# Second block's norms scaled inside their PSUM banks, next weight slabs split elsewhere, large SBUF buffers at multiples of 512 bytes

## The reference

```python
def layer_norm_2(x, g, b):
    xf = x.astype(jnp.float32)
    mu = jnp.mean(xf, axis=-1, keepdims=True)
    var = jnp.mean(jnp.square(xf - mu), axis=-1, keepdims=True)
    y = (xf - mu) * lax.rsqrt(var + LN_EPS)
    return (y * g.astype(jnp.float32) + b.astype(jnp.float32)).astype(x.dtype)

for l in range(DEPTH_2):
    mix = hybrid_mixer(h, w_in[l], ..., w_out[l], cos, sin)
    h = layer_norm_2(DEEPNORM_ALPHA * h + mix, ln1_g[l], ln1_b[l])
    h = layer_norm_2(DEEPNORM_ALPHA * h + cross_attention(h, mem, cq_w[l], ckv_w[l], co_w[l]),
                   ln2_g[l], ln2_b[l])
    h = layer_norm_2(DEEPNORM_ALPHA * h + swiglu(h, ffn_wi[l], ffn_wo[l]), ln3_g[l], ln3_b[l])
```

## Time and profile before

| | before |
|---|---|
| median of 3 runs | 2712.55 us |
| profiled execution | 2717.11 us |
| its span, first to last instruction | 2715.3 us |
| granted TensorE clock, mean | 0.978 of full speed |
| PE busy | 2594.8 us (96% of the span) |
| DVE, ACT, POOL busy | 1288.7, 1093.0, 885.8 us |
| HBM traffic | 317 MB, mean 117 GB/s |

### The profile page before, as it was taken

How to read it: one execution, slowest core, us unless ns; L and a number is a source line. 1 busy time by engine, 2 the same in 40 slices (tenths; PEclk the granted TensorE clock), 3 DMA queues, 4 the chain that set the end, 5 groups by cost and what they waited for, 6 DMA issues and landing times.

```text
span 2715.3 us, 30646 instructions
## 1 busy us (share of the span) xinstructions
PE 2594.8 (96%) x12190; PEld 2074.0 (76%) x12190; DVE 1288.7 (47%) x1823; ACT 1093.0 (40%) x1696; POOL 885.8 (33%) x390
## 2 busy tenths in 40 slices
PE   8988989999899999989999999999999999999997
PEld 6768787777776788877788888766888878788886
DVE  2994357777547557453431010576457353610113
ACT  3344236566337556333322222347374233322232
POOL 4470110000131344432244344322444432344344
PEclk9998989999999999999999999999999989999999
DMA  6232348899521233332223233221333331233232
GB/s 207 86 90 63 99 159 313 310 354 338 169 78 32 72 99 93 101 117 77 64 89 115 92 93 105 67 63 41 92 95 100 116 101 62 69 99 115 91 94 77
DMA packets 220077, 318.80 MB, mean 117 GB/s; under 512 B 17184, under 2 KB 176032, under 8 KB 219808
## 3 DMA queue, kind: packets, MB, share of 16 engines
q1 hardware_dynamic: 201184, 284.24, 32.6%
q10 hardware_dynamic: 16592, 24.72, 2.7%
q0 software_dynamic: 2160, 7.89, 0.8%
HBM read 301.06 MB, written 15.75 MB: 117 GB/s over the span
## 4 chain that ended last, share of the span: by engine, by line
PE 85%; DVE 10%; ACT 2%; issue 1%; DMA 1%; ACTq 0%; POOL 0%; DVEq 0%
PE ps L664 79%; PE ps L815 3%; PE ps L676 3%; DVE stats L2090 1%; DVE rows L2100 1%; DVE ix L2203 1%; DVE top L2201 1%; DVE pair_l L2377 1%; DVE x_lo L2016 1%; DVE shift L2119 0%; DMA rows<-in_x 0%; ACT w_hi L1463 0%; ACT pair_h L1694 0%; DVE rows L2112 0%; DVE qf L2468 0%
## 5 line engine op out<-in xcount | busy, mean ns | idle before, releaser
L605 POOL TENSOR_TENSOR w_lo<-w_raw,w_hi 128x1024 fp32r<-128x1024 f32 x331 | 814.2, 2471 | 1436.3 <-ACT w_hi L1463 1436.3
L664 PE MATMUL ps<-x_hi,w_hi 128*128 128x512 f32 x1624 | 656.1, 404 | 18.0 <-DVE x_lo L2016 15.5
L664 PE MATMUL ps<-x_lo,w_hi 128*128 128x512 f32 x1624 | 639.3, 394 | 0.0
L664 PE MATMUL ps<-x_hi,w_lo 128*128 128x512 f32 x1624 | 638.6, 393 | 0.0
L1463 ACT ACTIVATE w_hi<-w_raw 128x1024 fp32r<-128x1024 f32 x331 | 340.8, 1053 | 456.6 <-PE ps L664 449.4
L664 PEld LDWEIGHTS ps<-x_hi,w_hi 128*128 128x128 f32 x1624 | 307.7, 189 | 104.2 <-issue 19.4
L664 PEld LDWEIGHTS ps<-x_lo,w_hi 128*128 128x128 f32 x1624 | 307.6, 189 | 70.9
L664 PEld LDWEIGHTS ps<-x_hi,w_lo 128*128 128x128 f32 x1624 | 308.2, 190 | 66.2 <-issue 2.9
L2612 DVE TENSOR_TENSOR fhd<-fsg,ps 128x512 f32<-128x512 f32 x44 | 30.2, 687 | 391.5 <-PE ps L664 391.4
L2377 DVE TENSOR_TENSOR pair_l<-pair_raw,pair_h 128x2048 fp32r<-128x2048 f32 x84 | 189.8, 2287 | 47.1 <-ACT pair_h L1694 46.9
L1694 ACT ACTIVATE pair_h<-pair_raw 128x2048 fp32r<-128x2048 f32 x84 | 157.8, 1910 | 3.0 <-ACT yb L1709 2.8
(11 more groups left out here) (403 smaller groups left out, 4335.8 us busy)
## 6 DMA issues: line engine op xcount, KB each, us to landing
w_raw<-in_w_in SPq DMA_DIRECT2D x102, 512.0 KB, 3.7
w_raw<-in_ffn_wi SPq DMA_DIRECT2D x88, 512.0 KB, 3.5
pair_raw<-in_w_gate SPq DMA_DIRECT2D x56, 512.0 KB, 5.9
pair_raw<-in_w_up SPq DMA_DIRECT2D x56, 512.0 KB, 7.2
pair_raw<-in_w_down SPq DMA_DIRECT2D x56, 512.0 KB, 6.3
w_raw<-in_ffn_wo SPq DMA_DIRECT2D x44, 512.0 KB, 3.6
w_raw<-in_w_out SPq DMA_DIRECT2D x24, 512.0 KB, 3.6
kv_raw<-in_ckv_w SPq DMA_DIRECT2D x20, 512.0 KB, 4.1
```

What stands on the lines that cost most here:

```text
L605: pool.tensor_tensor(w_lo[:, slot, :], w_raw[:, slot, :], w_hi[:, slot, :].bitcast(F32), ALU.subtract).then_inc(lo_done, 1)
L664: ins = pe.matmul(o, a, b, start=first, stop=last)
```

## The change

**Norms.** For the six norms above DVE now scales each chunk in its bank (`ps[k] = ps[k]*gain + bias`, written back into PSUM), ACT copies the bank to `x_hi`, and DVE subtracts: `x_lo = ps[k] - x_hi`. DVE scales chunk k+1 ahead of the subtraction of chunk k. `vbuf` is no longer used for it. DVE waits for the gain's loads itself.

**Splits.** The slab after c is split before the first square root (`first`); the next two between the chunks of `x_hi`, after chunks 1 and 4. At the entry of the second block three slabs are still split ahead of all chunks. The six parameter loads at a layer's head come after the chunks, the fourth slab's split follows them ahead of the softplus, and one slab fewer is split after the second product.

**The tail of the row products.** Slab a is used by tiles 2 and 3 earlier: after c is taken the order is tile 2 with a, tile 0 with c, tile 3 with a (which releases a), tile 1 with c, then tile 2 with b and c. Before it was tiles 0 and 1 with c, tile 2 with a, b and c, and then tile 3 with a. For the last row product of the program (`final`) tiles 0 and 1 keep their places, and tile 3 with a comes ahead of tile 2 with b and c. The first half of the feed-forward part and the first block's row product take the new order too.

**Addresses.** The ring, the activations, the constants, `vbuf` and the arena of phase buffers now start at multiples of 512 bytes (before, 128, 192, 192, 448 and 384 bytes past one); small arrays were moved to the gaps.

```diff
@@ build: placement @@
+    def to_line():
+        top[0] = (top[0] + LINE - 1) // LINE * LINE
+        return top[0]
...
-    ring_at = top[0]
+    ring_at = to_line()
...
-    x_at = top[0]
+    x_at = to_line()
...
-    const_at = top[0]
+    const_at = to_line()
...
+    vbuf_at = to_line()
+    vbuf = place("vbuf", [P, 2, T])
...
-    arena = top[0]
+    arena = to_line()
@@ PE: rows_t @@
-                for t in (0, 1):
-                    both(t, single + 2, c)
-                for k, slot in ((single, a), (single + 1, b), (single + 2, c)):
+                if final:
+
+                    for t in (0, 1):
+                        both(t, single + 2, c)
+                    both(2, single, a)
+                else:
+                    both(2, single, a)
+                    both(0, single + 2, c)
+                both(3, single, a).then_inc(slab_used, 1)
+                if not final:
+                    both(1, single + 2, c)
+                for k, slot in ((single + 1, b), (single + 2, c)):
                     both(2, k, slot)
-                both(3, single, a).then_inc(slab_used, 1)
@@ ACT: normalise_tiles @@
+                if first is not None:
+                    first()
                 for t in range(NT):
@@ ACT: high parts @@
-            def norm_high_parts():
-                high_parts(x_hi, affine=lambda k: (gain_f[:, 0, k:k + 1], gain_f[:, 1, k:k + 1]))
+            def norm_high_parts(splits):
+
+                for k in range(KD):
+                    act.wait_ge(s["scaled"], done.at("scaled", k + 1))
+                    act.activation(x_hi[:, k, :], ps[:, k, :], ACT.Copy).then_inc(s["hi_ready"], 1)
+                    if splits and k in (1, 4):
+                        split(1)
+                done.passed(transposed=KD, scaled=KD)
@@ ACT: head of a layer @@
-                split(RING if l == 0 else RING - 1)
+                if l == 0:
+                    split(RING)
+                norm_high_parts(splits=l > 0)
                 load((taps[:, :, :], per_feature("conv_w_2", l)),
...
-                norm_high_parts()
+                split(1)
                 landed(6)
                 softplus(lam[:, 2, :], lam[:, 1, :], lam[:, 4, :], lam[:, 3, :])
...
-                        split(2)
+                        split(1 if j == 1 else 2)
@@ ACT: the norms after the mixer and the cross-attention @@
-                normalise_tiles(beside=lambda: split(1))
+                normalise_tiles(first=lambda: split(1))
                 done.passed(products=NT)
                 landed(6 + 4)
-                split(TAIL - 1)
-                norm_high_parts()
+                norm_high_parts(splits=True)
@@ DVE: low parts @@
-            def low_of_normed():
-
+            def low_of_normed(landed):
+
+                def low(k):
+                    dve.wait_ge(s["hi_ready"], done.at("hi_ready", k + 1))
+                    dve.tensor_tensor(x_lo[:, k, :], ps[:, k, :], x_hi[:, k, :].bitcast(F32), ALU.subtract)\
+                       .then_inc(s["lo_ready"], 1)
+
+                dve.wait_ge(s["params_landed"], done.at("params_landed", 16 * landed))
                 for k in range(KD):
-                    dve.wait_ge(s["hi_ready"], done.at("hi_ready", k + 1))
-                    link(dve.scalar_tensor_tensor(vbuf[:, k % 2, :], ps[:, k, :], gain_f[:, 0, k:k + 1],
-                                                  x_hi[:, k, :].bitcast(F32), ALU.mult, ALU.subtract))
-                    dve.tensor_scalar(x_lo[:, k, :], vbuf[:, k % 2, :], gain_f[:, 1, k:k + 1], None, ALU.add)\
-                       .then_inc(s["lo_ready"], 1)
-                done.passed(hi_ready=KD)
+                    dve.wait_ge(s["transposed"], done.at("transposed", k + 1))
+                    dve.tensor_scalar(ps[:, k, :], ps[:, k, :], gain_f[:, 0, k:k + 1], gain_f[:, 1, k:k + 1], ALU.mult,
+                                      ALU.add).then_inc(s["scaled"], 1)
+                    if k >= 1:
+                        low(k - 1)
+                low(KD - 1)
+                done.passed(hi_ready=KD, transposed=KD)
```

More of the change, by code:

```diff
@@ L54 @@
 SLAB, RING = 1024, 3
+LINE = 512
 TAIL = 3
@@ L738, in pair_f, with rows_t @@
                 used_later[0] = True
-            def rows_t(xh, xl, n, norm=True, tiles=(0, 1, 2, 3), ready=None):
+            def rows_t(xh, xl, n, norm=True, tiles=(0, 1, 2, 3), ready=None, final=False):
                 def part(t, k, slot, half):
@@ L1429, in hidden_for @@
                             pe.wait_ge(s["hidden_lo"], done.at("hidden_lo", c0 + k + 1))
[L1431 removed]
+                    rows_t(fh, fl, n, norm=half == 1, tiles=tiles, ready=hidden_for,
+                           final=half == 1 and l == LAYERS - 1)
                 done.passed(lo_ready=KD, first_half_summed=NT, silu_done=2 * pairs, hidden=2 * pairs, hidden_lo=2 * pairs,
@@ L1537, in load_norm, with normalise_tiles @@
                      (gain_f[:, 0, :], per_feature(g, l)), (gain_f[:, 1, :], per_feature(b, l)))
-            def normalise_tiles(beside=None, last=False):
+            def normalise_tiles(first=None, beside=None, last=False):
                 def normalise(t):
@@ L1966, in _ @@
                 assert slab.n == end
-                normalise_tiles(beside=(lambda: split(1)) if l < LAYERS - 1 else None, last=l == LAYERS - 1)
+                normalise_tiles(first=(lambda: split(1)) if l < LAYERS - 1 else None, last=l == LAYERS - 1)
                 done.passed(products=2 * NT, evacuated=18 + 8 + 8, gain_used=3, gates_full=2 * pairs, hidden=2 * pairs,
```

37 lines of the change are left out of this document (17 added, 20 removed).

## The result

| | before | after |
|---|---|---|
| median | 2712.92 us (2711.65 to 2714.28, 4 runs) | 2680.16 us (2673.25 to 2685.11, 4 runs) |
| profiled execution | 2717.11 us | 2685.11 us |
| its span, mean granted clock | 2715.3 us, 0.978 | 2683.3 us, 0.982 |

The recorded ratio is 0.9868 with a 95% interval of 0.9855 to 0.988, 1.3% less; the two medians of the table alone give 0.9879. The forecast was 2697 with a range of 2689 to 2706, so the sign was right and the size was not: 33 us came where 15 were forecast.

A forecast was written before the change was run, and what follows sets the result against it. PE is busy 96% of the span, so only its standstills could be won. Terms -11.9 - 0.9 + 1.4 - 1.8 + 0.1 - 2.0 = -15.1 us took the runs' median from 2712.55 to 2697, range 2689 to 2706.

The forecast's parts named there:

- The waits: Six norms: PE's waits for x_lo fall from 15.5 to 3.6 us, a gain of 11.9, with in-place scaling at 0.69.
- The shift: One-element DVE shift at L2119: its 1.54 us stall behind POOL goes, DVE starts 1.36 later; five norms gain 0.18 each.
- The feed-forward part's first half: PE waits 2.1 us there for POOL's low part of a slab; released 4.1 us sooner, 1.8 us won.
- The last norm: Last norm of all: tile 2 complete one step later, the shift just slips through ahead of POOL; costs 0.1 us.
- The head of a layer: Parameter loads behind the chunks: copies just in time, split half a slab late at most; cost 0, if wrong 1 to 2 us twice.
- Addresses. DVE and PE take no part in it that a row shows. Cost 0: New buffer addresses: no effect on DVE or PE, faster landing of loads worth nothing outside the experts; cost 0.
- rival 3: Experts: aligned loads speed them up, some 5 us at most, to 2692; chance 0.05.
- The clock. I take 0.5 each: Four norms: full clock back sooner where PE no longer stops between transposes and matmuls; 0.5 us each, 2.0 in all.
- Rival 2: The clock gives more, in four norms and PE's first matmuls at two warm norms: 4 to 6 us more, 2692; chance 0.12.
- The first block: Its norm had no stall to lose, so DVE's later start loses 1.36 us; sign: tile 3 normalised 14.4 us after tile 0's start.
- Rival 5: Norms' chunks: in-place scaling takes twice the row, 1.4 us, eating the gain from 1.25 on; 22 us slower, 2719; chance 0.05.
- A DVE instruction whose operands all lie in SBUF waits: Norms: while POOL works, such an instruction waits for it; one with an input in PSUM does not.

The follow-up runs named there:

- dist0: The kernel before with x_hi and x_lo moved from 192 to 128 bytes past a multiple of 512, everything else at its old place past one: 2702.82 us, ratio 0.995.
- fill_before: The kernel before with transposes of tile 0 repeated where PE waits for the normalised tiles, changing no value: 2716.86 us, ratio 1.0002.
- late_start: The changed kernel with PE's first matmul after a norm held until the third chunk's x_lo instead of the first: 2702.29 us, ratio 0.9956.
- old_splits: The changed kernel with the slabs split at their old places: 2681.66 us, ratio 0.9874; repeated, 2683.19 us, ratio 0.9884.

## Why the forecast was off, and what in it held

- **The waits: right.** `x_lo` 4.4 us against 3.6 forecast. The shift at 0.16 in five norms was exact, and so was the 0.18 a norm, within 0.01. The in-place scaling took 0.811 us, not the 0.692 of the earlier trace rows that I took. A chunk therefore comes every 1.32 us (0.72 of scaling, 0.60 of subtraction), which the reckoning had at 1.3.
- **The feed-forward part's first half: right**, 1.5 of 1.8. **The last norm: right**, nothing; its second shift stood 0.92 us beside POOL. **The head of a layer: right**, PE has no wait there.
- **"Addresses. DVE and PE take no part in it that a row shows. Cost 0": the step that failed**, by 12.4 us of the 17.6 by which the account exceeds the forecast. PE does take part: its matmuls step by 0.2267 us in place of 0.2289 once both operands start at the same place modulo 256 bytes. I bounded the term by the loads, the only user of addresses that I had thought of, and made them rival 3. In the experts, where the loads are dense, the whole gain is 3 us, 2.6 of it is the same shorter step, and `dist0` has it with loads that are not aligned. (Nor is every load of that rival a 4 KB row: of the 35661 packets from 400 to 700 us, 13628 are under 2 KB.) The trace of before could have told, though no group of rows shows it: in one stretch of the kernel before the products of `x` step by 0.2289 and the row products by 0.2267. I took 0.227 from the earlier trace rows, a mean over both, and called it the pace of a matmul.
- **"The clock. I take 0.5 each": the term that was mis-sized.** It measured 1.27 in each of five norms and some 1 at the entry, 7.4 us in place of 2.0. Rival 2 had named the place (the first matmuls after a warm restart run slowly) and a size of 4 to 6 us more, where 5.4 came; I gave it 0.12. What I held against it, the long wait for the last tile, turned out not to matter: `fill_before` filled it and won nothing.
- **The first block: term right, price not.** The row product's end to the last normalisation went from 3.98 to 5.35 us, 1.37 where 1.36 was forecast; the sign I named for it, 14.4 us from tile 0, was the wrong measure, since the chain itself stayed 13.09 and only began later. Another 1.66 us was half clock after its restart, which is chance there. From the row product's end to the 96th matmul the six profiles with the old order have 28.3 us each time; of the eight with the new order five have 31.3 to 31.6, and three (`late_start`, `old_splits` and its repeat) have 28.0 to 28.2.
- **Rival 5** needed 1.25 us for the scaling; with 0.81 it was far off.
- **"A DVE instruction whose operands all lie in SBUF waits" for POOL: too wide, without a cost here.** In the last norm of the changed kernel POOL works from 2665.04 to 2667.43, and two statistics over SBUF rows, from 2665.55 on, take the 1.29 us that they take elsewhere. What waited in these runs was the `SCALAR_TENSOR_TENSOR` of one element (0.16 to 1.70 us) and the `TENSOR_SCALAR` of 512 (0.49 to 2.59).

## What to carry to other kernels

Read the step between matmuls operand by operand in a stretch without waits, and if two kinds of full-size matmul differ by a per cent, look at where their operands start: here the distance between the moving and the stationary operand, modulo 256 bytes, is worth up to 3% of a matmul's step (0.2267 to 0.2335 us) and costs a few hundred bytes of padding. A wait removed right ahead of PE's restart was worth more than its length here, since the matmuls behind it ran at full clock: 2.0 us of waiting put back cost 4.2 a norm. Before splitting work "beside" a chain on another engine, list which of the chain's instructions have all operands in SBUF, see in a trace which of those wait, and put the POOL operation after the last of them. Then test the order as a whole: the split ahead of the roots needed the early release of slab a, while the old order with the split behind the last root was 10 us faster than both together.

## What the hardware showed that was not expected

- The Trainium skill, TensorE: Matmul & The Clock Gate, section Wait — 56ns, not 53.3ns?, gives one figure for back-to-back matmuls of 512 columns at the full clock, 215.7 ns. Here they step by 0.2267, 0.2289, 0.2323 to 0.2335 or 0.2332 to 0.2335 us for distances of 0, 64, 128 and 192 bytes modulo 256; the measurement decides. Places of 32, 96 and 160 past a multiple gave 0.2334, 0.2336 and 0.2342 with the stationary operand at 0.
- DVE scales 512 elements within a PSUM bank in 0.811 us, where PSUM to SBUF takes 0.692; ACT's copy out of the bank beside it takes 0.60.
- Two profiled executions of one program differ by 8.1 us, nearly all of it in a few stretches at half clock; in the second block everything between them repeats to 0.01 us.
